# Ones-matmuls over constants in the waits of the norm entries of a fused two-block transformer kernel

## The chip, the cores and the metric

The kernel runs on 1 core of one Trainium2 chip. The metric is the device time of one execution in microseconds (us); the time before is the median of 3 runs. In the profile TensorE is called PE (its weight loads PEld), VectorE DVE, ScalarE ACT, GpSimd POOL and SyncE SP.

## The reference, cut to what matters

Two transformer models of two layers each run one behind the other over 256 tokens (272 with 16 meta tokens in the first), model width 1024, all in float32. What the change touches is the normalisation in front of a projection, with the residual added just before it:

```python
def rmsnorm(x, g):
    xf = x.astype(jnp.float32)
    y = xf * lax.rsqrt(jnp.mean(xf * xf, axis=-1, keepdims=True) + EPS)
    return (y * g.astype(jnp.float32)).astype(x.dtype)
...
    for l in range(DEPTH):
        g = norm_gains[l]
        hn = rmsnorm(h, g[0])
...
        h = h + rmsnorm(mix, g[1])
        ff = conv_ffn(rmsnorm(h, g[2]), ffn_w_up[l], ffn_conv[l], ffn_w_down[l])
        h = h + rmsnorm(ff, g[3])
```

## The kernel before, in words

Activations stand transposed in SBUF: 1024 features are 8 tiles (k = 0 to 7) of 128 partitions, with up to 272 token columns. A weight item is 2048 columns wide (two output tiles of 8 blocks). It is loaded by SP into one of four slots `raw`, ACT copies it to `w_hi` in the fp32r format (line 220), DVE makes the remainder `w_lo` (line 224), and TensorE multiplies three times for each block: w_hi by x_hi, w_hi by x_lo, w_lo by x_hi (lines 412 to 414 in a `Product`; 1078 to 1080, 1455 to 1457 and 1908 to 1910 in the mixers). Each engine runs its own program in order; semaphores tie them together. The stages of the program are blocks with a barrier of all engines between them (lines 464, 815 and 840 in the profile).

The class `NormEntry` stands at the start of five stages. Its order of work:

- With a residual that is itself normalised (four of the five entries: feed-forward 0, the attention mixer "fox", feed-forward 1, the delta-rule mixer "gdn"), ACT takes the square root of the sum that the stage before has left in bank 7 (line 658), DVE inverts it (line 689), and then for each k DVE scales the branch (line 709) and adds it to `h` (line 694).
- ACT squares each `h` tile as it is added (line 664) into `work`.
- TensorE sums the squares over the partitions: for each k it waits for `squared` and does one plain float32 matmul with a block of ones as the stationary operand, accumulating in bank 6 (lines 738 to 740). The last one raises `summed`.
- ACT takes the root (line 668), DVE inverts (line 689), and then for each k DVE applies the gain (line 726), ACT makes x_hi (line 678 or 676), DVE makes x_lo (line 704 or 702). The product behind the entry waits for x_lo of each k in its first tile.

The fifth entry, the very first one of the program (mixer "hgrn"), has no residual: `h` comes by DMA and ACT squares its tiles one behind the other. There ACT then splits one weight item (`act_first`), and after x_hi it splits three more before it copies out the first product tiles (line 1262).

`consts` holds the identity in columns 0 to 127, ones in columns 128 to 255 and a causal mask in the next 128, all float32. Bank 3 is written and read by no instruction of these entries; the mixers use it only later in their own stages.

Of the kernel before, what the change touches and what calls it, by code (L numbers as in the profile page):

```python
# [23 lines left out]
P = 128  # L24
# [82 lines left out]
def fused_model(nc, w, params_d, consts_d, hT_d, c_d, pos_d, out_d):  # L107
    with ExitStack() as ctx:
        def sbuf(c, name, shape, dt=F32):
            return c.enter_context(nc.sbuf_tensor(name, shape, dt))  # L110

        params = sbuf(ctx, "feature_params", [P, NPARAM])
        consts = sbuf(ctx, "constants", [P, NHELD])
# [11 lines left out]
        bank = [ctx.enter_context(nc.psum_tensor(f"bank{i}", [P, 512], F32)) for i in range(8)]  # L125
# [13 lines left out]
        def con(name, c0=0, n=None, p0=0, p1=P):  # L139
            n = dict(CONSTS)[name] - c0 if n is None else n  # L140
            return consts[p0:p1, CCOL[name] + c0:CCOL[name] + c0 + n]

        ident, ones = con("ident"), con("ones")
# [384 lines left out]
        class Streamed:  # L528
# [99 lines left out]
            def passed(self):  # L628
                for s_, n_ in self.counts:
                    s_.passed(n_)  # L630

        class NormEntry:


# [4 lines left out]
            def __init__(self, src, n, cols, gain, x_hi, x_lo, shift=None, residual=None, stats=True, count=D,  # L639
# [94 lines left out]

                def pe(pe):
                    if stats:
                        for k in range(n):
                            pe.wait_ge(squared.sem, squared.at(k + 1))
                            last = pe.matmul(bank[6][:, 0:c1 - c0], ones, work[:, k, c0:c1], start=k == 0,
                                             stop=k == n - 1)  # L740
                        last.then_inc(summed.sem, 1)
                self.act, self.dve, self.pe = act, dve, pe

            def passed(self):
# [2250 lines left out]
```

## Time and profile before

| what | value |
|---|---|
| time before, median of 3 runs | 1592.12 us |
| lowest and highest of the 3 | 1586.9 and 1592.16 us |
| the profiled execution, its own time | 1594.11 us |
| span of the profile | 1592.3 us |
| TensorE busy | 1470.3 us, 92% |
| VectorE busy | 1042.5 us, 65% |
| ScalarE busy | 781.4 us, 49% |
| mean granted TensorE clock | 0.961 of full speed |

The profiled execution took 1594.11 us, of which the span of its instructions is 1592.3 us; 1.8 us lie around it. The granted clock (PEclk) is 1.00 for 2.4 GHz and 0.50 for 1.2 GHz; a value between them in a stretch means that it held both levels. A matmul record is longer than the distance to the next one, since matmuls are pipelined: the rate of a stream is read from the starts. One plain float32 matmul of the program appears as two records.

### The profile page before, as it was taken

The numbers are of one execution on the slowest core, as the hardware profiler recorded it, in microseconds if no ns is written. First come the engines' busy times: TensorE is split into PE (matmuls) and PEld (weight loads), VectorE is DVE, ScalarE is ACT, GpSimd is POOL, SyncE is SP. The second block draws the span as 40 slices with busy tenths as digits, with TensorE's granted clock in tenths as the row PEclk, the third lists the DMA queues.
The fourth block names the chain that finished last, engine by engine and source line by source line (L and its number), as shares of the span: only waits on it lengthen the run. The fifth ranks groups of instructions, "written<-read, shape, count | busy, mean of one in ns | idle before, by whom it ended". The sixth has DMA issues, their size and how long they took to land. (4 is left out here: it accounts for less than half of the span.)

```text
span 1592.3 us, 29023 instructions
## 1 busy us (share of the span) xinstructions
PE 1470.3 (92%) x11301; PEld 1407.4 (88%) x11301; DVE 1042.5 (65%) x1727; ACT 781.4 (49%) x1272; POOL 283.8 (18%) x384
## 2 busy tenths in 40 slices
PE   5999879999797898999997899989999988999997
PEld 4999769999686677899996789989999987899997
DVE  5564678877774546788757754457887665687643
ACT  5655644554354444555545565565433555554341
POOL 0000102120053430121100153202333100123210
PEclk8999889999998899999998999999999998999999
DMA  7432526659532224465772311135775733365451
GB/s 281 166 129 106 187 95 221 231 170 349 187 123 90 80 84 182 159 219 207 253 257 82 133 54 54 54 126 209 264 270 202 244 123 133 106 258 219 143 180 47
DMA packets 41140, 265.80 MB, mean 167 GB/s; under 512 B 4560, under 2 KB 5712, under 8 KB 15440
## 3 DMA queue, kind: packets, MB, share of 16 engines
q1 hardware_dynamic: 41040, 264.44, 45.7%
q8 instruction: 65, 1.06, 0.3%
q14 instruction: 35, 0.29, 0.0%
HBM read 263.38 MB, written 1.05 MB: 166 GB/s over the span
## 5 line engine op out<-in xcount | busy, mean ns | idle before, releaser
L224 DVE TENSOR_TENSOR w_lo<-raw,w_hi 128x2048 fp32r<-128x2048 f32 (+2 forms) x207 | 425.8, 2062 | 236.5 <-ACT w_hi L220 233.4
L220 ACT ACTIVATE w_hi<-raw 128x2048 fp32r<-128x2048 f32 (+3 forms) x224 | 386.1, 1728 | 37.4 <-PE bank L414 33.4
L412 PE MATMUL bank<-x_hi_up,w_hi 128*128 128x272 f32 (+1 forms) x704 | 203.7, 289 | 8.2 <-DVE x_lo_up L704 8.1
L414 PE MATMUL bank<-x_hi_up,w_lo 128*128 128x272 f32 (+1 forms) x704 | 202.2, 287 | 0.0
L413 PE MATMUL bank<-x_lo_up,w_hi 128*128 128x272 f32 (+1 forms) x704 | 201.7, 287 | 0.0
L412 PE MATMUL bank<-z_hi,w_hi 128*128 128x258 f32 x704 | 200.3, 285 | 0.0
L413 PE MATMUL bank<-z_lo,w_hi 128*128 128x258 f32 x704 | 198.7, 282 | 0.0
L414 PE MATMUL bank<-z_hi,w_lo 128*128 128x258 f32 x704 | 198.0, 281 | 0.0
L412 PEld LDWEIGHTS bank<-x_hi_up,w_hi 128*128 128x128 f32 x704 | 133.7, 190 | 9.9 <-issue 8.8
L413 PEld LDWEIGHTS bank<-x_lo_up,w_hi 128*128 128x128 f32 x704 | 134.2, 191 | 0.0
L414 PEld LDWEIGHTS bank<-x_hi_up,w_lo 128*128 128x128 f32 x704 | 133.9, 190 | 0.0
L413 PEld LDWEIGHTS bank<-z_lo,w_hi 128*128 128x128 f32 x704 | 133.3, 189 | 0.1
L414 PEld LDWEIGHTS bank<-z_hi,w_lo 128*128 128x128 f32 x704 | 132.6, 188 | 0.0
L412 PEld LDWEIGHTS bank<-z_hi,w_hi 128*128 128x128 f32 x704 | 132.3, 188 | 0.1
L412 PE MATMUL bank<-a_hi_up,w_hi 128*128 128x272 f32 (+1 forms) x352 | 102.9, 292 | 0.0
L414 PE MATMUL bank<-a_hi_up,w_lo 128*128 128x272 f32 (+1 forms) x352 | 100.2, 285 | 0.0
L413 PE MATMUL bank<-a_lo_up,w_hi 128*128 128x272 f32 (+1 forms) x352 | 100.1, 285 | 0.0
L412 PE MATMUL bank<-a_hi_gu,w_hi 128*128 128x256 f32 x352 | 98.8, 281 | 1.2 <-DVEq L576 1.2
L413 PE MATMUL bank<-a_lo_gu,w_hi 128*128 128x256 f32 x352 | 98.6, 280 | 0.0
L414 PE MATMUL bank<-a_hi_gu,w_lo 128*128 128x256 f32 x352 | 98.6, 280 | 0.0
L953 ACT ACTIVATE act_gu<-z_gu 128x256 f32<-128x256 f32 x44 | 22.6, 513 | 144.8 <-DVE z_gu L944 144.8
L1908 PE MATMUL bank<-x_hi_e,w_hi 128*128 128x256 f32 x264 | 80.8, 306 | 8.0 <-DVE x_lo_e L702 4.1
(456 smaller groups left out, 3914.6 us busy)
## 6 DMA issues: line engine op xcount, KB each, us to landing
raw<-w_up SPq DMA_DIRECT2D x44, 1024.0 KB, 4.8
raw<-w_gu SPq DMA_DIRECT2D x44, 1024.0 KB, 4.8
work<-w_ada SPq DMA_DIRECT2D x27, 1024.0 KB, 5.0
raw<-w_down SPq DMA_DIRECT2D x32, 704.0 KB, 4.4
raw<-w_dn SPq DMA_DIRECT2D x32, 704.0 KB, 4.1
raw<-w_a_in SPq DMA_DIRECT2D x16, 1024.0 KB, 5.4
mod_w_down<-w_ada SPq DMA_DIRECT2D x12, 1024.0 KB, 6.0
raw<-w_gdn_qkv SPq DMA_DIRECT2D x12, 1024.0 KB, 4.8
```

Source lines behind the costliest of these rows:

```text
L220: act.activation(w_hi[:, s, 0:blocks * P], raw[:, s, 0:blocks * P], ACT.Copy).then_inc(hi_split.sem, 1)
L224: dve.tensor_tensor(w_lo[:, s, 0:blocks * P], raw[:, s, 0:blocks * P], w_hi[:, s, 0:blocks * P].bitcast(F32), ALU.subtract).then_inc(lo_sp ...
L412: pe.matmul(o, w_hi[:, s, b], x_hi[:, xk, cols[0]:cols[1]], start=begin, stop=False)
L413: pe.matmul(o, w_hi[:, s, b], x_lo[:, xk, cols[0]:cols[1]], start=False, stop=False)
L414: last = pe.matmul(o, w_lo[:, s, b], x_hi[:, xk, cols[0]:cols[1]], start=False, stop=end)
L953: act.activation(act_s[:, s % 2, :], z[:, 2 * (s % 2), 0:SEQ], ACT.Silu, bias=z[:, 2 * (s % 2), SEQ:SEQ + 1]).then_inc(silued.sem, 1)
L1908: pe.matmul(o, w_hi[:, s, w_], x_hi[:, k_, :], start=k_ == 0, stop=False)
```

## The change

A helper `spin` issues n plain float32 matmuls of the ones block over the first columns of the constants into bank 3, which nobody reads and for which nobody waits. In each entry with a residual, eight of 256 columns stand ahead of the wait for the first square. In all five entries one of 128 columns stands behind each of the first seven sums, and seven of 256 columns stand behind the last sum, ahead of the product.

```diff
+        def spin(pe, n, columns):
+            for _ in range(n):
+                pe.matmul(bank[3][:, 0:columns], ones, consts[:, 0:columns], start=True, stop=True)
...
                 def pe(pe):
                     if stats:
+                        if residual:
+                            spin(pe, 8, 2 * P)
                         for k in range(n):
                             pe.wait_ge(squared.sem, squared.at(k + 1))
                             last = pe.matmul(bank[6][:, 0:c1 - c0], ones, work[:, k, c0:c1], start=k == 0,
                                              stop=k == n - 1)
+                            if k < n - 1:
+                                spin(pe, 1, P)
                         last.then_inc(summed.sem, 1)
+                        spin(pe, 7, 2 * P)
```

## Rows read from the trace of the kernel before

**Rows 1.** The page: busy time and share of the span of each engine.

```profile
PE 1470.3 (92%) x11301; PEld 1407.4 (88%) x11301; DVE 1042.5 (65%) x1727; ACT 781.4 (49%) x1272; POOL 283.8 (18%) x384
```

**Rows 2.** Stretches at feed-forward 0: stretch, length, busy by engine, clock, DMA share, GB/s.

```profile
200.00:202.00 2.00, 0.90 (x4) 0.30 (x2) 0.37 (x2) 0.61 (x2) 0.00 (x0) 1.00 0.89 377
206.00:208.00 2.00, 2.00 (x6) 1.47 (x5) 2.00 (x7) 1.00 (x4) 0.00 (x0) 0.50 0.00 0
210.00:212.00 2.00, 1.59 (x7) 0.95 (x5) 0.00 (x0) 0.65 (x2) 0.00 (x0) 1.00 0.00 0
218.00:220.00 2.00, 2.00 (x9) 1.93 (x9) 2.00 (x6) 1.04 (x3) 0.00 (x0) 0.50 0.00 0
```

**Rows 3.** Timeline, feed-forward 0: start, duration, engine, line, instruction, idle before and its releaser.

```profile
198.65 2.24 PE L433 MATMUL bank<-branch_sq_a_out,constants 128*128 128x272 f32 x8
201.20 0.49 ACT L658 ACTIVATE std<-bank,eps_col 128x272 f32<-128x272 f32 x1 [1.08 <-PEq L464]
205.39 6.20 PE L739 MATMUL bank<-work,constants 128*128 128x272 f32 x16 [4.49 <-ACT work L664]
209.49 0.79 ACT L664 ACTIVATE work<-h 128x272 f32<-128x272 f32 x2 [0.33 <-DVE h L694]
211.63 0.49 ACT L668 ACTIVATE std<-bank,eps_col 128x272 f32<-128x272 f32 x1 [1.35 <-PE bank L739]
215.70 0.36 PE L412 MATMUL bank<-x_hi_up,w_hi 128*128 128x272 f32 x1 [4.10 <-DVE x_lo_up L704]
219.70 1.03 DVE L704 TENSOR_TENSOR x_lo_up<-work,x_hi_up 128x272 fp32r<-128x272 f32 x2
220.78 0.39 PE L412 MATMUL bank<-x_hi_up,w_hi 128*128 128x272 f32 x1
```

**Rows 4.** Timeline, ACT: root behind the sums in fox, feed-forward 1 and gdn.

```profile
433.67 0.49 ACT L668 ACTIVATE std<-bank,eps_col 128x272 f32<-128x272 f32 x1 [1.18 <-PE bank L739]
...
637.32 0.48 ACT L668 ACTIVATE std<-bank,eps_col 128x258 f32<-128x258 f32 x1 [2.14 <-PE bank L739]
...
847.11 0.47 ACT L668 ACTIVATE std<-bank,eps_col 128x256 f32<-128x256 f32 x1 [0.89 <-PE bank L739]
```

**Rows 5.** Timeline, PE: unbroken streams of plain float32 matmuls of 272, 256, 128 columns.

```profile
159.47 3.93 PE L784 MATMUL bank<-qfig,constants 128*128 128x272 f32 x16 [1.20 <-ACT qfig L764]
901.81 1.13 PE L1936 MATMUL bank<-gate_rows,constants 128*128 128x256 f32 x4 [2.54 <-DVE gate_tok L2114]
1021.28 0.61 PE L1985 MATMUL bank<-constants,qkvg 128*128 128x128 f32 x4
```

**Rows 6.** The half-clock stretches of four entries, the sum row of eight.

```profile
sum 47.70, PE 37.63 PEld 32.03 DVE 42.95 ACT 24.23 POOL 0.49; mean PE 4.70 PEld 4.00 DVE 5.37 ACT 3.03 POOL 0.06
```

**Rows 7.** Timeline: last x_lo, and matmul 48 of the first item, feed-forward 1 and gdn.

```profile
645.09 1.00 DVE L704 TENSOR_TENSOR x_lo_up<-work,x_hi_up 128x258 fp32r<-128x258 f32 x2
649.75 0.28 PE L414 MATMUL bank<-x_hi_up,w_lo 128*128 128x258 f32 x1
855.96 0.48 DVE L702 SCALAR_TENSOR_TENSOR x_lo_e<-work,mod,x_hi_e 128x256 fp32r<-128x256 f32 x1 [0.18 <-ACT x_hi_e L676]
860.57 0.28 PE L1910 MATMUL bank<-x_hi_e,w_lo 128*128 128x256 f32 x1
```

**Rows 8.** Timeline, first entry.

```profile
11.47 5.89 PE L739 MATMUL bank<-work,constants 128*128 128x272 f32 x16 [11.47 <-ACT work L664]
17.40 0.49 ACT L668 ACTIVATE std<-bank,eps_col 128x272 f32<-128x272 f32 x1 [0.63 <-PE bank L739]
17.92 1.85 DVE L689 RECIPROCAL rstd<-std 128x272 f32<-128x272 f32 x1
33.21 0.56 PE L1078 MATMUL bank<-x_hi_a,w_hi 128*128 128x272 f32 x1 [3.08 <-ACT qfig L1262]
```

**Rows 9.** Two stretches of 6 us behind the first entry, columns as in rows 2.

```profile
33.20:39.20 6.00, 5.99 (x26) 6.00 (x27) 4.75 (x6) 2.13 (x3) 0.00 (x0) 0.50 0.96 360
39.20:45.20 6.00, 6.00 (x50) 6.00 (x49) 2.15 (x5) 2.43 (x3) 0.00 (x0) 0.99 0.61 239
```

## The prediction

> **What bounds the kernel now.** I read the page first: TensorE is busy 92% of the span [rows 1], so a microsecond in which it waits, or works at the lower clock with nothing else ahead of it, is a microsecond of the result. Then I cut the surroundings of the entry of feed-forward 0 into short stretches [rows 2]. TensorE goes into the entry at a granted clock of 1.00 (2.4 GHz), works at 0.50 (1.2 GHz) from 206 to 208 us, has 1.00 again from 210, and 0.50 once more from 218 to 220. In the timeline [rows 3] it ends the last sum of the stage before at 200.89, idles 4.49 us until the first square, sums from 205.39 to 211.59, idles 4.10 us until the first x_lo, and then follows the x_lo tiles. So each entry has two idle stretches, and the clock falls behind each. The other three residual entries show the same two falls; the eight half-clock stretches (203.2 to 210.0, 216.8 to 220.3, 425.1 to 431.9, 438.7 to 442.1, 629.9 to 636.7, 640.1 to 646.9, 838.1 to 844.9, 851.7 to 858.5) are 47.7 us together [rows 6].
>
> What matters is what ends last in them. Up to the last square DVE and ACT set the pace: the h additions and squares come about 0.77 us apart. The chain feels TensorE only through the delay from the last square to the root on ACT, which is ACT's idle time there: 1.35 us at feed-forward 0 [rows 3], 1.18 in fox, 2.14 at feed-forward 1, 0.89 in gdn [rows 4]. In the product, DVE makes an x_lo every 0.77 us. At feed-forward 0 the last is ready at 220.73, and TensorE starts on it at 220.78 [rows 3], although its clock was 0.50 just before: no lag, so that fall cost nothing.
>
> **Prices of the added work.** A float32 stream of 272 columns has 16 records in 3.93 us, first start to last end; less one record of about 0.39 and a late first one this is 0.23 us a record, 0.46 a matmul (two records). The 256-column stream gives (1.13 - 0.38) / 3 = 0.22 after taking out a slow first record, 0.43 to 0.5 a matmul; the 128-column one (0.61 - 0.27) / 3 = 0.11, 0.22 a matmul [rows 5]. Half clock doubles them: 0.92, 0.87 and 0.44 us. The rows behind the first entry show that factor: 26 matmuls in 6 us at 0.50 and 50 in 6 us at 0.99 [rows 9].
>
> **Ahead of the squares (eight of 256).** 8 x 0.43 = 3.5 us at full clock. Cover: from about 201.20, when the barrier lets ACT go, to 205.39 there are 4.2 us [rows 3]. It fits with 0.7 us over; the other three have 4.0 to 4.1 us. Price 0 as long as the clock is still 1.00 when it begins, which it is [rows 2]. At half clock throughout it would be 7.0 us, 2.8 late.
>
> **Between the sums (seven of 128).** A sum and a filler are 0.46 + 0.22 = 0.68 us, under the 0.77 us of a square, so there is no backlog at full clock. The last two squares, however, come closer (two of 0.43 us in 0.79, 0.36 apart [rows 3]); there sum, filler and sum (1.14 us) begin 0.36 us before the last square is done, and with some 0.25 us from the last matmul to ACT the root follows the last square by about 1.05 us. The nearest row without a filler is gdn's 0.89 us, whose last sums ran at full clock [rows 4]. Expected change of the delay: 1.35, 1.18, 2.14 and 0.89 become 1.05 each, so -0.30, -0.13, -1.09 and +0.16, together -1.4 us if the clock holds.
>
> **Behind the sums (seven of 256).** 7 x 0.43 = 3.0 us, in an idle stretch of 4.10 us [rows 3]. Price 0; at half clock 6.1 us, some 2 us too long. About 1.1 us of idleness stays.
>
> **In the product.** Here a held clock pays only where TensorE lags behind the last x_lo. From its end to the 48th matmul of the first item, 27 matmuls, there are at full clock about 27 x 0.12 = 3.2 us (3.1 with 256 columns) [rows 9]. Feed-forward 1 took 649.75 - 646.09 = 3.66, gdn 860.57 - 856.44 = 4.13 [rows 7]: 0.4 and 1.0 us to gain, nothing in the other two. TensorE is only about half busy while it follows DVE's x_lo, so the clock may still fall in some entry; I take 1.1 of the 1.4 us.
>
> **The first entry.** It has no spin ahead, and its squares are all done at 13.7 us, so TensorE is what ends last: its sums take 5.89 us, ACT's root starts at 17.40 as they end, and the inversion at 17.92 right behind [rows 8]. Seven fillers lie wholly on that chain. At full clock they cost 7 x 0.22 = 1.5 us, at half 3.1. Eight sums at the full rate would be 3.7 us; 5.89 says that half of them ran at the lower one (the columns, the profile's clock for the very beginning being an unrecorded 1.00). The clock rises at the same time in both kernels, and the seven fillers lengthen the part after the rise: +1.5 us. Nothing absorbs it, since TensorE's next wait (3.08 us before 33.21) is for ACT, whose work follows from the same x tiles.
>
> **Sum.** +1.5 - 1.4 - 1.1 = -1.0 us. The profiled execution took 1594.11 us, 2.0 above the median of 1592.12; from the median the sum gives 1591.1. The clock falls elsewhere too, for example 6 us at half rate behind the first entry [rows 9], which cost 3 us; whether such a fall comes depends on small shifts in time, and the three runs before spread over 5.3 us. I put 4 us either way on that: own range 1587 to 1595.
>
> **Rivals.**
> - *Half clock is lost time.* If all 47.7 us counted, holding 1.00 would give back 23.9 us: 1568. The rows speak against it: 7 us of half clock or idleness at a time left delays of 1 or 2 us, and none where TensorE follows DVE [rows 3, 4, 7]. The Trainium skill (TensorE: Matmul & The Clock Gate, section Terms) prices the penalty as throttled time times one less the clock ratio; by it the time would be those 1568 us, and the rows above disagree. Chance 3%.
> - *The spin does not hold the clock* (its side is slower). Repeated ones and an identity might not count as work. Then the clock falls at 203.2 as before: 2.0 us of spin at full rate, the rest at half, to 206.2, 0.8 late; a sum and a filler take 1.36 us until the rise at 210.0, that is 2.8 pairs, and 5.2 more at 0.68 end at 213.5 instead of 211.59. Each residual entry loses 1.9 us, 7.6 in all, and with the first entry's 1.5 it is 9.1: 1601. It decides from the point where a pair costs more than 0.77 us. Against it: the sums themselves, the same instruction with ones, brought the clock back at 210 [rows 2]. Chance 7%.
> - *As that, and the fillers keep it from rising at all.* Eight pairs at 1.36 us end at 216.8, the spin behind them 6.1 us later at 222.9, and the product starts 7 us late: 28 us, with 3 for the first entry 1623. Chance 3%.
> - *The cover ahead of the squares is too short*, TensorE leaving the barrier 1 us behind ACT: 0.3 to 0.5 us an entry, 2 us together: 1593. It lies inside my range.
>
> **How the numbers follow.** My forecast has 87%, the rivals 3, 7 and 3%. A measurement of this kernel tells about 0.5% (8 us) from no change. Faster (under 1584.2): 3% for the first rival. Slower (over 1600.1): half or more of the second, and the third: 7%. The same: 90%. For eight times in ten the own range would nearly do; to take in the edge of the second rival and the fall of clock elsewhere it is 1585 to 1599.
>
> **What the profile after should show.** Granted clock 1.00 from 203 to 217 us; spin records ended by about 204.8 and 214.4; ACT's idle before line 668's root near 1.05 us in the four entries; matmul 48 at 3.2 us behind the last x_lo; the first entry's root near 18.9 us. I am wrong if the clock is 0.50 in those stretches with the spin running, if the root comes over 1.5 us behind the last square, or if the mean granted clock rises clearly over 0.961 and the time falls by over 8 us.

## The result

The changed kernel took 1596.39 us (median of 11 runs, 1592.73 to 1598.57) against 1591.26 us for the kernel before on the same chip (11 runs, 1586.42 to 1592.63): ratio 1.0033, 95% interval 1.0024 to 1.0042. That is 5.1 us slower, within the 0.5% that I called the same, and inside my range of 1585 to 1599 (the own range, 1587 to 1595, is missed by 1.4), but clear of the noise of so many runs and on the other side of zero from my sum (-1.0 us). The changed kernel was timed three more times below and was 3.2, 1.5 and 3.6 us slower in the medians; over all four, 47 runs have a median of 1593.87 us and the 106 of the kernel before 1590.28, so 3.6 us (3.1 in the means).

**The profile after.** The span is 1596.8 us, the execution's own time 1598.57, its mean granted clock 0.973 where it was 0.961. First the page, then stretches around feed-forward 0, which begins some 1.5 us earlier than in [rows 2].

```profile
PE 1501.7 (94%) x11505; PEld 1431.2 (90%) x11505; DVE 1043.0 (65%) x1727; ACT 781.0 (49%) x1272; POOL 281.6 (18%) x384
```

```profile
200.00:202.00 2.00, 2.00 (x11) 1.77 (x10) 1.83 (x1) 0.14 (x1) 0.00 (x0) 1.00 0.10 41
206.00:208.00 2.00, 2.00 (x13) 1.78 (x12) 2.00 (x7) 1.00 (x4) 0.00 (x0) 1.00 0.04 8
210.00:212.00 2.00, 2.00 (x11) 1.77 (x10) 1.54 (x1) 0.36 (x1) 0.00 (x0) 1.00 0.00 0
218.00:220.00 2.00, 1.88 (x14) 1.50 (x12) 0.81 (x3) 0.43 (x1) 0.00 (x0) 1.00 0.12 16
```

TensorE is busy 31 us longer and has 204 matmul records more, two for each of the 102 added matmuls, and the clock is 1.00 in the stretches where it was 0.50 in [rows 2]. The timeline of the same entry, against [rows 3]:

```profile
199.65 0.49 ACT L662 ACTIVATE std<-bank,eps_col 128x272 f32<-128x272 f32 x1 [1.08 <-PEq L464]
199.67 3.69 PE L634 MATMUL bank<-constants 128*128 128x256 f32 x16 [0.32 <-PEq L464]
203.84 0.72 PE L745 MATMUL bank<-work,constants 128*128 128x272 f32 x2 [0.48 <-ACT work L668]
207.94 0.78 ACT L668 ACTIVATE work<-h 128x272 f32<-128x272 f32 x2 [0.34 <-DVE h L698]
209.87 0.49 ACT L672 ACTIVATE std<-bank,eps_col 128x272 f32<-128x272 f32 x1 [1.15 <-PE bank L745]
209.67 3.19 PE L634 MATMUL bank<-constants 128*128 128x256 f32 x14
213.93 0.36 PE L412 MATMUL bank<-x_hi_up,w_hi 128*128 128x272 f32 x1 [1.08 <-DVE x_lo_up L708]
217.94 1.02 DVE L708 TENSOR_TENSOR x_lo_up<-work,x_hi_up 128x272 fp32r<-128x272 f32 x2
```

TensorE leaves the barrier with ACT (199.67 and 199.65), its eight spins end at 203.36, the first sum starts at 203.84, the seven behind end at 212.86 and the product starts at 213.93. Both spins are hidden here as priced. ACT waits 1.15 us from the last square to the root (line 672), where it was 1.35 in [rows 3] and I expected 1.05.

The roots of the other three entries, answering to [rows 4], and the spin ahead in fox:

```profile
432.38 0.49 ACT L672 ACTIVATE std<-bank,eps_col 128x272 f32<-128x272 f32 x1 [1.57 <-PE bank L745]
...
639.02 0.48 ACT L672 ACTIVATE std<-bank,eps_col 128x258 f32<-128x258 f32 x1 [1.11 <-PE bank L745]
...
849.29 0.47 ACT L672 ACTIVATE std<-bank,eps_col 128x256 f32<-128x256 f32 x1 [1.76 <-PE bank L745]
```

```profile
421.74 5.38 PE L634 MATMUL bank<-constants 128*128 128x256 f32 x16 [0.99 <-PEq L464]
```

Feed-forward 1 has 1.11 us in place of 2.14. Fox has 1.57 (1.18 before) and gdn 1.76 (0.89 before): there the clock fell under the spin ahead, which took 5.38 us in place of 3.7, so that in fox the sums began 1.1 us behind the end of the first square, and in gdn 1.3. Both delays are over the 1.5 us that the prediction named as a sign of being wrong. The four delays add up to 5.59 us, where they were 5.56.

The first entry, answering to [rows 8]:

```profile
11.35 1.27 PE L745 MATMUL bank<-work,constants 128*128 128x272 f32 x2 [11.35 <-ACT work L668]
12.41 0.64 PE L634 MATMUL bank<-constants 128*128 128x128 f32 x2
...
14.17 1.11 PE L745 MATMUL bank<-work,constants 128*128 128x272 f32 x2
15.08 0.63 PE L634 MATMUL bank<-constants 128*128 128x128 f32 x2
15.51 1.08 PE L745 MATMUL bank<-work,constants 128*128 128x272 f32 x2
...
17.33 0.62 PE L745 MATMUL bank<-work,constants 128*128 128x272 f32 x2
17.79 0.38 PE L634 MATMUL bank<-constants 128*128 128x128 f32 x2
18.01 0.62 PE L745 MATMUL bank<-work,constants 128*128 128x272 f32 x2
...
19.15 3.19 PE L634 MATMUL bank<-constants 128*128 128x256 f32 x14
```

A sum and its filler take 15.51 - 14.17 = 1.34 us at the lower level and 18.01 - 17.33 = 0.68 at the upper one, within 0.02 us the prices of the prediction. (Which level it is, I read from the rate: the trace has no record of the clock before 16.4 us here, and prints 1.00.) The sums run from 11.35 to 19.32, 7.97 us in place of 5.89: +2.1 us on the chain in this pair of profiles. Part of it is that the rate doubled later here, at 16.4 us and not at 15.5; more on that below.

### The profile page after: what moved, and what is told of

Same layout as the page of the kernel before. It is cut to its first block and busy times, and to the rows that moved or that the text cites. A ratio compares the mean times of both kernels' runs of the same rounds, so it can differ in the third digit from the quotient of the medians.

```text
span 1596.8 us, 29431 instructions
## 1 busy us (share of the span) xinstructions
PE 1501.7 (94%) x11505; PEld 1431.2 (90%) x11505; DVE 1043.0 (65%) x1727; ACT 781.0 (49%) x1272; POOL 281.6 (18%) x384
## 3 DMA queue, kind: packets, MB, share of 16 engines
HBM read 263.38 MB, written 1.05 MB: 166 GB/s over the span
```

## The experiments

Each group of kernels was timed beside the kernel before on one chip. Unless a number is given, a kernel had 12 runs; the interval in brackets is the 95% interval of the ratio. The kernels differ only in the spins. "Delay" is ACT's idle time from the last square to the root.

**The kernel before, again (again).** No edit.

> The kernel before, unchanged, timed against itself: ratio 1.000 within 0.1%. Its profile is a second draw of where the clock falls. The theory that the places of the falls outside the entries are luck: they differ from the first profile, and the total of half-clock time outside the entries differs by 5 to 30 us between the two. The theory that they are fixed by the program: the same falls at the same places, to 3 us.

1589.89 us against 1590.38, ratio 1.000 (0.999 to 1.0009). Its roots in the four residual entries:

```profile
207.46 0.49 ACT L668 ACTIVATE std<-bank,eps_col 128x272 f32<-128x272 f32 x1 [0.94 <-PE bank L739]
...
429.36 0.49 ACT L668 ACTIVATE std<-bank,eps_col 128x272 f32<-128x272 f32 x1 [1.05 <-PE bank L739]
...
633.77 0.48 ACT L668 ACTIVATE std<-bank,eps_col 128x258 f32<-128x258 f32 x1 [1.25 <-PE bank L739]
...
843.16 0.47 ACT L668 ACTIVATE std<-bank,eps_col 128x256 f32<-128x256 f32 x1 [0.89 <-PE bank L739]
```

The delays are 0.94, 1.05, 1.25 and 0.89, together 4.13 us; in the profile on which I predicted they were 5.56. The clock falls at the entries here too, but at other moments of them. Outside the entries the trace has 68 us of half clock, and the first profile 75: 7 in place of 17 us in hgrn, 27 in place of 24 in fox, 30 in both in the long rest. That is the expected sign of luck, near the lower end of the 5 to 30 us. The span is 4.7 us shorter, with the same instructions. So the whole 1.4 us that I meant to gain in these delays is what two executions of one kernel differ by.

**The first entry alone (first_only), the residual entries alone (residual_only).**

```diff
-                            if k < n - 1:
+                            if not residual and k < n - 1:
                                 spin(pe, 1, P)
...
-                        spin(pe, 7, 2 * P)
+                        if not residual:
+                            spin(pe, 7, 2 * P)
```

and no spin ahead. The other kernel has `residual` in both conditions and keeps the spin ahead.

> The change in the first entry alone (seven fillers of 128 columns, seven spins of 256 behind the last sum), the four residual entries as before. Theory A (the fillers of the first entry lie on its chain and cost about 2 us in the profile, the rest is small): 1.5 to 2.5 us slower, ratio 1.001 to 1.0016. Theory B (the loss of 5 us comes with the residual entries or with what the clock does after them): under 1.5 us here. Theory C (the first entry is nearly all of it, through what its delay shifts): 4 to 5 us slower, ratio about 1.003.

> The change in the four residual entries alone, the first entry as before. Theory A: the delays of the root gain nothing in sum and the product halves give back 1 us, so -1 to +1.5 us. Theory B (the held clock in the entries is paid back by falls in later stages, in fox and gdn above all): 3 to 5 us slower, ratio 1.002 to 1.003, and the loss appears in the trace behind the entries and not in them. Theory C: within 1 us of the kernel before.

First entry alone: 1593.53 us against 1590.38, ratio 1.0018 (1.0008 to 1.0029). Residual entries alone: 1591.94, ratio 1.0012 (0.9999 to 1.0026). Some 3 us for the one and 1.6 for the other; the interval of the second touches 1. Its delays are 1.15, 1.15, 1.12 and 1.76, 5.18 us in all, between the 4.13 and the 5.56 of the two profiles of before, so no gain is seen there.

**Spins without fillers (no_fillers).**

```diff
-                            if k < n - 1:
-                                spin(pe, 1, P)
```

> The spins ahead and behind as in the changed kernel, the fillers between the sums left out in all five entries. Theory A: the first entry costs nothing and the roots follow the last square 0.2 us sooner, so the time is 0 to 2 us under the kernel before. Theory B (the clock outside the entries): still 2 to 4 us slower. Theory C (first entry, fillers): within 1 us of the kernel before.

1590.31 us against 1590.38, ratio 1.0001 (0.9991 to 1.001), that is -1.4 to +1.6 us. The delays:

```profile
209.97 0.49 ACT L672 ACTIVATE std<-bank,eps_col 128x272 f32<-128x272 f32 x1 [0.93 <-PE bank L745]
...
431.81 0.49 ACT L672 ACTIVATE std<-bank,eps_col 128x272 f32<-128x272 f32 x1 [0.92 <-PE bank L745]
...
635.84 0.48 ACT L672 ACTIVATE std<-bank,eps_col 128x258 f32<-128x258 f32 x1 [0.89 <-PE bank L745]
...
845.25 0.47 ACT L672 ACTIVATE std<-bank,eps_col 128x256 f32<-128x256 f32 x1 [0.89 <-PE bank L745]
```

0.93, 0.92, 0.89 and 0.89: 0.22 us under the 1.15 and 1.11 of the same entries with fillers and the clock held. A filler in front of the last sum costs its own length, since the last two squares come close together. Without the fillers the loss is gone.

**Fillers alone, in the first entry (fill_first) and in the residual ones (fill_only).** As no_fillers turned round: `spin(pe, 1, P)` under `if not residual and k < n - 1` or `if residual and k < n - 1`, and no other spin.

> Only the seven fillers of 128 columns between the sums of the first entry; no other spin anywhere. Theory F: 1.5 to 3 us slower, all of it in the first entry's sums (7.0 to 8.5 us long where they were 5.5 to 5.9). Rival (the spin behind the first entry's sums is the loss there): within 1 us of the kernel before.

> Only the fillers between the sums of the four residual entries; no spins ahead or behind, first entry as before. Nothing holds the clock here when the sums begin. By my price of a sum and a filler at half clock (1.36 us against 0.77 for a square) the root comes 2.5 to 3.5 us behind the last square wherever the clock is at 0.50 through the sums, 1.9 us more than before per entry, 4 to 8 us slower in all. If half clock prices are wrong (theory: a filler hides in the wait for the next square at either clock), within 1.5 us of the kernel before.

First entry: 1592.30 us against 1590.14, ratio 1.001 (0.9997 to 1.0023). That is 2.2 us slower, but the interval includes 1 and the rival's 1 us, so the time alone does not decide. The profile shows the sums 7.15 us long without any spin behind them, against 7.32 in first_only; the spin behind is not needed to explain what the first entry loses. Residual entries (6 runs): 1601.48 us, ratio 1.0068 (1.005 to 1.0087), 11.3 us slower, more than the 4 to 8 expected.

```profile
210.76 0.49 ACT L672 ACTIVATE std<-bank,eps_col 128x272 f32<-128x272 f32 x1 [2.32 <-PE bank L743]
...
435.42 0.49 ACT L672 ACTIVATE std<-bank,eps_col 128x272 f32<-128x272 f32 x1 [3.21 <-PE bank L743]
...
643.12 0.48 ACT L672 ACTIVATE std<-bank,eps_col 128x258 f32<-128x258 f32 x1 [3.52 <-PE bank L743]
...
854.93 0.47 ACT L672 ACTIVATE std<-bank,eps_col 128x256 f32<-128x256 f32 x1 [3.32 <-PE bank L743]
```

With nothing to hold the clock, the delays are 2.32, 3.21, 3.52 and 3.32, 12.4 us together: 8.2 more than in the second profile of the kernel before (again), 7.5 more than the mean of four such profiles (4.9, below). This is the mechanism of my second rival (a pair costs 1.36 us at half clock against 0.77 for a square), here without a spin ahead. The remaining 3 to 4 us were not traced to a place.

**Fillers doubled (double_fill).**

```diff
                             if k < n - 1:
-                                spin(pe, 1, P)
+                                spin(pe, 2, P)
```

> The changed kernel with two fillers of 128 columns between the sums in place of one, in all five entries. Theory F: the first entry's sums 1.5 to 2.5 us longer again; in the others sum and two fillers take 0.46 + 0.44 = 0.90 us against 0.77 for a square, so the root comes about 2.0 to 2.3 us behind the last square in place of 1.15: 4 us. In all 5 to 7 us over the changed kernel, 10 to 12 over the kernel before. If fillers are not the loss: 0 to 2 us over the changed kernel.

1596.98 us (8 runs) against 1590.14, ratio 1.0038 (1.0022 to 1.0053): 6.8 us over the kernel before, less than the 10 to 12 expected, since I had counted them on top of the first timing of the changed kernel; over the changed kernel of the same group (1593.35) it is 3.6, where I had 5 to 7. In the profile the parts are as priced: delays 2.21, 2.20, 2.22 and 2.22, the first entry's sums 9.16 us. Against the means of the profiles that have no spins in those entries or no fillers in the first (4.9 and 6.1, below) that is 4.0 us in the delays and 3.0 in the sums, 7.0 for the 6.8 measured.

**The changed kernel three more times (changed_again, changed_third, changed_fourth).**

> The changed kernel once more, unchanged. Theory F (the fillers are the loss: about 2 to 3 us in the first entry, about 2 us in the four others): 4 to 6 us over the kernel before; the roots of the four entries 1.1 us behind the last square where the clock was held, the first entry's sums near 8 us long. Theory P (the placing of the clock falls in fox made the first profile and the timing slow): the fox entry to the feed-forward 1 entry takes 203 to 205 us here and the median is within 2 us of the kernel before.

> The changed kernel a third time, unchanged. Both profiles of it so far have the stage of fox (product end of its entry to the next entry's first root) at 184.3 us and the rest behind the gdn entry at 734.6, where the kernel before has 180.3 and 181.9, and 731.8. Theory P (where the clock falls lie in fox and gdn is part of the loss, and it repeats): 184 and 734 to 735 again, time 3 to 5 us over the kernel before. If it is luck from execution to execution: fox 180 to 182 or the rest 730 to 732 here, and the pooled median of the three timings 2 to 3 us over the kernel before.

> The changed kernel a fourth time. The three timings so far are 5.1, 3.2 and 1.5 us over the kernel before in the medians. Theory F+P (2.0 us in the first entry, 0.2 us in the four others taken together, and the rest from where the clock happens to fall in fox and behind gdn, which differs between executions): 1 to 5 us over, pooled 2.5 to 3.5. Rival (the first timing was right, a fixed loss of 5 us): 4.5 to 5.5 us over.

1593.35 against 1590.14, ratio 1.0011 (0.9996 to 1.0026); 1592.01 against 1590.49, 1.0011 (0.9999 to 1.0023); 1593.64 against 1590.01, 1.0022 (1.001 to 1.0034). Two of the three intervals end below 5 us (4.1 and 3.7; the third at 5.4), and over all four timings the difference of the means is 3.1 us, give or take 1: a fixed loss of 5 us is not supported. The placing of the falls in fox does not repeat.

The table has the lengths of the stages in each profile, from matmul 48 of one entry's product to the next entry's first root, each a difference of two starts in the timeline. Behind the length of hgrn, of the entries and of fox stands, in brackets, how many us of it the trace has at half clock.

| profile | to matmul 48 of the first entry | hgrn | four residual entries, first root to matmul 48, sum | fox | behind gdn's matmul 48 | span |
|---|---|---|---|---|---|---|
| before | 29.85 | 171.35 (17) | 92.06 (48) | 180.27 (24) | 731.75 | 1592.3 |
| again | 29.44 | 168.01 (7) | 89.31 (38) | 181.92 (27) | 731.88 | 1587.6 |
| changed, first | 31.80 | 167.85 (7) | 91.17 (10) | 184.28 (34) | 734.57 | 1596.8 |
| changed_again | 31.58 | 167.80 (7) | 91.19 (10) | 184.26 (34) | 734.64 | 1596.5 |
| changed_third | 32.11 | 168.03 (7) | 89.70 (0) | 181.76 (27) | 731.97 | 1590.7 |
| changed_fourth | 32.03 | 167.96 (7) | 89.66 (0) | 181.72 (27) | 729.08 | 1587.6 |
| no_fillers | 30.46 | 169.50 (10) | 88.81 (3) | 181.91 (27) | 731.37 | 1589.2 |
| spins_short | 30.03 | 169.11 (10) | 88.77 (3) | 181.85 (27) | 733.30 | 1590.2 |

The two feed-forward stages are left out; they have no half clock, and each keeps its length within 0.1 us in all profiles. The first column goes by the kernel: over all 18 profiles 31.4 to 32.1 with one filler between the sums, 29.4 to 30.8 without. Fox and the rest do not: the same instructions take 181.7 or 184.3 us, and 729.1 to 734.6. In fox the length follows the half clock: 180.3, 181.8, 183 and 184.3 us with 24, 27, 31 and 34 us of it, in all 18 profiles within 0.4 us, so each us of half clock there costs about 0.4 us (0.3 in hgrn). In the residual entries the same price does not hold: spins_short has 3 us of it and takes 88.8 us, again has 38 and takes 89.3, so 35 us of half clock cost 0.5 us. Only the last ones, up to the 48 us and 92.1 us of the first profile, cost as in fox. That is the difference between a stage that TensorE bounds and one in which DVE and ACT set the pace until a backlog builds up.

The clock of one stretch around fox shows it too, in the first profile of the changed kernel and then in changed_fourth (columns as in [rows 2]):

```profile
421.50:628.50 207.00, 185.46 (x1231) 158.25 (x1231) 118.10 (x300) 97.40 (x246) 68.63 (x116) 0.91 0.29 108
```

```profile
421.50:628.50 207.00, 184.15 (x1240) 157.09 (x1241) 119.78 (x304) 97.50 (x247) 68.69 (x116) 0.93 0.31 111
```

0.91 against 0.93 of 207 us is about 4 us of full-rate work; the first execution needs 207.45 us from the first root of fox to that of feed-forward 1 (421.72 to 629.17), the other 204.46 (422.05 to 626.51). What makes the clock fall more often in one execution than in another of the same binary stays open.

**Pure delay before fox (delay_fox_2, delay_fox_4).**

```diff
                             pe.wait_ge(squared.sem, squared.at(k + 1))
+                            if k == n - 1 and residual and len(residual) > 2:
+                                spin(pe, 2, 2 * P)
```

where fox's `residual` has a third element, and with 4 in the other kernel.

> The changed kernel with two more ones-matmuls of 256 columns just ahead of the last sum of the fox entry, on its chain: 0.9 us of pure delay before fox. Theory P: the stage of fox no longer takes 184.3 us but 180 to 182.5, or the rest behind the gdn entry changes by over 1 us, so that the time does not move by the 0.9 us but by -3 to +1. Theory N (the later stages do not depend on when they begin): fox 184.3 +-0.3, rest 734.6 +-0.3, time +0.9 us against the changed kernel.

> The same with four: 1.7 us of pure delay before fox. Theory P: fox and the rest take other lengths than 184.3 and 734.6 us, by 1 us or more, and the time moves by something between -3 and +3. Theory N: fox 184.3, rest 734.6, time +1.7 us against the changed kernel.

1593.03 us, ratio 1.0017 (1.0004 to 1.0031), and 1593.39 us, ratio 1.0025 (1.0013 to 1.0038), beside the 1592.01 of the changed kernel in the same group: 1.0 and 1.4 us for 0.9 and 1.7 us of delay. The runs of one kernel spread over 8 to 10 us, so each difference is known only to about 2 us. In the profiles the delay to fox's root grew by 0.86 and 1.72 us (2.01 and 2.87 against 1.15), fox took 182.98 and 180.54 us and the rest 729.92 and 734.27. So theory N's fixed lengths are wrong, the later stages do vary, and the medians show no loss beyond the delay itself. Theory P explains single executions; as a cause of a fixed loss nothing here supports it.

**Which spin is worth something (pre6_only, post_only), and the version left over (spins_short).** Six spins ahead alone; seven behind alone; both, in the residual entries, without fillers and with the first entry untouched:

```diff
                         if residual:
-                            spin(pe, 8, 2 * P)
+                            spin(pe, 6, 2 * P)
...
-                            if k < n - 1:
-                                spin(pe, 1, P)
...
-                        spin(pe, 7, 2 * P)
+                        if residual:
+                            spin(pe, 7, 2 * P)
```

> Only the six spins ahead of the squares in the four residual entries; no fillers, nothing behind the sums. The clock is held through the sums, so the roots follow the last square by 0.9 us in the four entries, about 1.2 us less than before in sum; behind the sums TensorE idles 4 us again, so the clock falls in the products and matmul 48 is 3.2 to 4.1 us behind the last x_lo as before. 0.5 to 1.5 us faster.

> Only the seven spins behind the sums in the four residual entries. The roots stay 0.9 to 2.1 us behind the last square as before; in feed-forward 1 and gdn matmul 48 comes 3.2 us behind the last x_lo. The clock may be at 0.50 when the sums end, so that the spin is up to 6.1 us long against 4.1 us of cover and delays the product where that happens: between 0.5 us faster and 2 us slower.

> The version the experiments point to: residual entries alone, six spins of 256 columns ahead of the squares (2.6 us at full clock, so that they are not late where the clock falls under them), seven behind the sums, no fillers; first entry as before. By the sums of the entries (roots 0.9 us behind the last square in all four, product at 3.2 to 3.4) it should be 1 to 1.5 us faster than the kernel before, ratio 0.999 to 1.000, which this measurement can hardly tell. If the clock falls during the sums in some entry, the gain is lost: 0 to 1 us slower.

> The version with six spins ahead, seven behind, no fillers and the first entry left alone, a second time. It was 1.7 us under the kernel before, interval -0.24% to +0.03%. Its entries together are 1.7 us shorter in the profile. If that is real: 1 to 2.5 us under again. If the interval's upper end is right: within 0.5 us.

pre6_only: 1591.51 against 1590.01, ratio 1.0003 (0.9991 to 1.0016), the delays 0.92, 0.93, 0.89 and 0.88 as expected, the time no different. post_only: 1592.87, ratio 1.0015 (1.0005 to 1.0025), 2.9 us slower, more than I allowed; its delays of 0.92, 0.93, 1.22 and 2.14 are no worse than before and matmul 48 comes 3.3 us behind the last x_lo in feed-forward 1 and gdn, so the profile does not show where these 2.9 us are (its interval, 0.8 to 4.0 us, leaves out zero). spins_short: 1588.77 against 1590.49, ratio 0.9989 (0.9976 to 1.0003), and on the second timing 1590.78 against 1590.01, ratio 1.0003 (0.9992 to 1.0014). With no_fillers it has the shortest entries of all (88.8 us in the table, delays 0.92, 0.92, 0.89, 0.88), 0.5 us under again and 3.3 under before, and no gain that the timings confirm: over both of them it is 0.3 us under the kernel before in the means, give or take 1.2.

## Why the prediction went wrong

**The change part by part.** Right: at feed-forward 0 the spins ahead and behind lie in idle time (3.69 and 3.19 us against 4.2 and 4.1 us of cover) and the clock is held; TensorE leaves the barrier with ACT (0.02 us apart there and in fox), which excludes the fourth rival; and the prices of 0.68 and 1.36 us a pair were measured as 0.68 and 1.34. The price of a 256-column matmul was right too, 0.43 us, though the quotient printed for it, (1.13 - 0.38) / 3, gives 0.25 a record and not 0.22; the spin ahead has (3.69 - 0.38) / 15 = 0.22. The first rival is excluded by the runs: in the group of no_fillers the mean granted clock of an execution rose from 0.966 (35 of the kernel before) to 0.978 (12) and the time did not move, where time lost in proportion would have given 0.012 x 1590 = 19 us. The Trainium skill (TensorE: Matmul & The Clock Gate, section Terms) prices half clock that way; these runs disagree with it for stretches in which another engine sets the pace.

**The step that failed is "Between the sums".** It forecast -1.4 us, from delays before (1.35, 1.18, 2.14, 0.89) that it took from one execution. Four profiles whose residual entries are as before (before, again, first_only, fill_first) have 5.56, 4.13, 5.40 and 4.43 us in sum, mean 4.9; the four of the changed kernel have 5.59, 5.62, 4.52 and 4.52, mean 5.1. Measured change: +0.2 us. Both of its terms were mis-sized. The delays before came from an unlucky execution, 0.7 us over the mean of the four, and I had no second one to see it by, though the three times before spread over 5.3 us. And the delay after is not 1.05 but 1.11 to 1.15 with the clock held, and 1.57 to 1.77 where it falls under the spin ahead, which I had called free "as long as the clock is still 1.00 when it begins". In fox and gdn TensorE has two waits of 0.8 and 1.0 us ahead of the spin, and in two of four executions the clock fell within 1 us of its start. Even a held clock would have brought the mean of 4.9 only to 4.5. This step is off by 1.6 us and the next one by 0.9, together 2.5 of the 4.1 to 4.6 us between my sum and the measurement.

**"In the product"** has the same fault: 1.1 us to be gained from 3.66 and 4.13 us. The floor was right (3.2 to 3.3 us with the clock held), the start was not. Over the same four and four profiles, the two lags together are 7.79, 6.49, 6.85 and 6.47 (mean 6.9) against 6.86, 6.89, 6.49 and 6.48 (6.7): -0.2 us.

**"The first entry"** was right in mechanism and in size: it is the one fixed part of the loss. The comparison of the two profiles above, +2.1 us, overstates it. How long the sums take depends also on when their rate doubles, where the trace's record of the clock begins: between 14.4 and 17.3 us in the 18 profiles, and each us later makes them about 0.5 us longer, with fillers and without. The four profiles of the changed kernel happened to have late rises (sums of 7.97, 7.83, 8.35 and 8.23 us). A pair with the same start and the same rise, near 16.9 us, is no_fillers (first line) and changed_fourth (its first and its last sum):

```profile
11.32 6.67 PE L745 MATMUL bank<-work,constants 128*128 128x272 f32 x16 [11.32 <-ACT work L668]
```

```profile
11.32 1.27 PE L745 MATMUL bank<-work,constants 128*128 128x272 f32 x2 [11.32 <-ACT work L668]
...
18.93 0.62 PE L745 MATMUL bank<-work,constants 128*128 128x272 f32 x2
```

The sums take 6.67 us in the one and 8.23 in the other: +1.6 us. All eight profiles with one filler between these sums (the changed kernel four times, first_only, fill_first and the two with a delay before fox) have a mean of 7.67 us, the nine without fillers there 6.12: +1.55, with the same mean time of the rise. Forecast was 1.5. Where fillers ran at the lower level, they moved sums behind the rise, as the prediction had it.

**The sum** is then +1.6 + 0.2 - 0.2 = +1.6 us, against 3.1 to 3.6 us over 47 and 106 runs. The fillers carry all of what is explained: left out, the loss is gone (no_fillers); doubled, it is 6.8. What stays open is the last 1.5 to 2 us. In the table hgrn is 1.8 us shorter in the changed profiles than in the mean of before and again, and fox 1.9 us longer, but these are few draws. With every profile in which the entry ahead of the stage has the spins of the changed kernel (in fox also the two with a delay) set against those in which it is as before, the differences are -0.8 us (7 and 8 profiles) and +1.4 (7 and 4), and the same instructions vary by 2 to 3 us from execution to execution, so neither is shown to be the kernel's. Open too is why post_only lost 2.9 us. The first timing's 5.1 us was at the high end: later timings gave less.

**The second rival**, the clock not held, came true for the changed kernel only in part: under the spin ahead in two entries of two profiles. The third, a clock that never rises, did not occur. What fillers do where nothing holds the clock, fill_only shows: 2.3 to 3.5 us of delay in each entry, 7.5 us more together than in the mean of the four profiles above, which is the 7.6 that I had for the four entries, but 11.3 us in the time.

## What to carry to other kernels

Before filling TensorE's idle time to hold its clock, ask what ends last in the stretch: where VectorE or ScalarE feed it tile by tile, half clock costs only the backlog behind the last tile, here 0 to 1.3 us at the sums of an entry and 0 to 0.9 in its product, however many microseconds of half clock the profile shows; where TensorE itself sets the pace, it cost 0.3 to 0.4 us for each. Spins in front of a wait with cover showed no cost in the profiles and no gain in the time (and post_only was slower for a reason not found); work put between instructions of a chain costs its full length where the operands are already there (the first entry) and before the last link (the two close squares). The length of a piece that the clock rises in should be compared between executions with the same time of the rise. And a wait of 1 or 2 us that depends on when the clock fell must be read from several executions before it enters a sum.

## What the runs showed of the hardware

The same binary took 1585.97 to 1594.4 us over the runs of the kernel before, and its two profiles differ by 4.7 us in span: the granted clock falls at different moments of the same instruction stream, and the lengths of single stages (hgrn 168.0 and 171.4, fox 180.3 and 181.9) follow.

Plain float32 matmuls of ones over constants, with nothing else running on TensorE, kept the clock at 1.00 at feed-forward 0 through waits behind which it had been at 0.50 before. They did not always: in fox and gdn it fell under them in two of the four profiles of the changed kernel.

Mean granted clock was no guide to time between kernels: 0.978 with no_fillers at 1590.3 us, 0.980 with double_fill at 1597.0, 0.966 with the kernel before at 1590.4. Within one kernel it was: over 142 runs of the kernel before and 47 of the changed one, the correlation of clock and time is -0.86 and -0.89, and a run with 0.01 less clock took 9 to 10 us more. What differs between runs of one kernel is half clock in stages like fox, which costs time; what the spins took away was half clock in waits for other engines, which cost little until a backlog builds up (0.5 us for the 35 us between spins_short and again).
